# Gram products of the two heads side by side in the array's rows, and twelve slots for the experts' loaded tiles

## The chip, the core and the metric

The program runs on one core of a Trainium2 chip. The metric is the time of one execution on the device, in microseconds (us); lower is better. The core's engines run their own instruction streams and meet at semaphores: TensorE (PE, with the weight loads shown apart as PEld), VectorE (DVE), ScalarE (ACT), GpSimd (POOL), and SyncE (SP), which here issues nearly all loads. PE, DVE and ACT work out of two on-chip memories: SBUF, into which loads go, and PSUM, eight banks of 128 rows by 512 fp32 numbers, into which PE writes.

## The reference, cut to what matters

Two transformer blocks in fp32 run one behind the other on 256 tokens of width 1024. The change touches one stage in each. In the first block it is the mixture of experts, 4 groups of 8 experts, every expert with three matrices of 1024 x 256, 1024 x 256 and 256 x 1024:

```python
for g in range(N_GROUPS):
    hid = jax.nn.silu(jnp.einsum("bld,edf->blef", h, w_gate[g])) * jnp.einsum("bld,edf->blef", h, w_up[g])
    out = out + jnp.einsum("blef,ble,efd->bld", hid, comb[:, :, g], w_down[g])
```

`comb` is zero but for two experts of one group per token. In the second block it is the RWKV-7 mixer, a recurrence over tokens with 16 heads of 64. The kernel computes it in chunks of 128 tokens (two chunks, t = 0 and 1): products of decayed keys and queries within a chunk (the Gram products), the inverse of a triangular 128 x 128 matrix from them, and a 64 x 64 state per head that goes from the first chunk to the second.

## The kernel before

**Tiles of weights.** All large matrices are streamed through one ring in quarters of 128 x 1024 fp32 (512 KB). They are numbered through the program: `Q_MOE` = 84 is the first of the experts' 192, `Q_PLE` = 276 the first behind them. SP loads quarter n into a raw slot (`load`, L262). ACT writes its rounded high half to `whi` (`split_high`, L269), and DVE or POOL writes the rest to `wlo` (`split_low`, L275). `whi` and `wlo` have four slots. PE then does three products for one of fp32 (`times`, L282), at lines L284 to L286, and L1443 to L1445 for the experts' second matrix. Each product has 512 columns. The raw ring has four slots, and six during the experts (`MOE_RING`); the two more are carved from `proj`, whose end is free by then. `load` waits until the low half of the quarter that was in the slot is made: n - 6 for the experts, n - 4 elsewhere. So loads run six quarters, one expert, ahead of the splits. One semaphore per slot (`raw_full`) counts landed transfers; two transfers of 256 KB make one quarter of an expert.

**The experts.** The router's stage comes first (L1223 to L1376): norm, transposes, logits, a small product with `w_ple`, the choice of tokens. ACT issues seven loads for it after the last product of the first mixer (`router_loads`, L1210). `sp_experts` (L1190) issues the first four quarters, waits for the first quarter of the output product, and loops over the groups. For expert E, PE does gate and up of expert E+1 (four quarters), turns the hidden tile of E with two transposes (L1431), and then does down of E (two quarters). ACT copies the turned hidden tile (L1511) and does the silu (L1507); DVE splits all 192 quarters and multiplies. Once per group of 8 experts the tokens of the next group are gathered (L1387, `dve_gather`, L1409) and the group's result is scattered back (L1493, L1501).

**The heads.** `pe_heads`, `act_heads` and `dve_heads` (L2204, L2414, L2528) work on eight pairs of heads, the first by itself (`first`), six in a loop and the last by itself. A `step` (L2319) inverts for pair p in seven levels: `below` (L2254, masked by DVE at L2595) and `grow` (L2268 and L2272, copied by ACT at L2439 and L2440). Between the levels it does the tail of pair p-1 (`rest`, `solve`, `state`, `outputs`) and prepares pair p+1: `decays` (L2210), `turn_ar`, `turn_bk`, and behind `grow` of level 5 and `below` of level 6 the two calls of `grams` (L2238). The heads of a pair lie on rows 0 to 63 and 64 to 127 of `AR` and `BK`. A unit is one head and one chunk, numbered 2h + t, so the first call has both chunks of head 0 and the second those of head 1. Units alternate between banks 5 and 4, and each of the second call waits until DVE has masked the unit that was in its bank. DVE's `mask_grams` (L2573) does two units at L2576 and then two steps on both (L2585, L2588), the second of which the next pair's `below` of level 0 waits for. `decays` of the next pair waits for all four masks, since it writes bank 4. DVE's order is: mask level 5, centre pair p-1, mask units 0 and 1, mask level 6, mask units 2 and 3.

The pair's state is `SB`, 128 x 128 with a block for each head. In the second chunk `rest` and `outputs` multiply by it, 64 columns for each head at a time (L2284, L2312). For pair 0, `first` puts the two calls of `grams` behind the quarters 5 and 6 of the projection of the convolution (`Q_CONV`). The last loads ahead of the heads are three rows at L1802, which DVE waits for ahead of step 0 (`rows_loaded`).

## Time and profile before

| | us |
|---|---|
| three timed runs, median | 1567.47 (1564.97 to 1572.5) |
| the profiled execution | 1559.74 |
| its span, from the first to the last instruction | 1557.9 |
| PE busy | 1395.5 |
| DVE busy | 867.3 |
| ACT busy | 723.3 |
| POOL busy | 609.6 |
| experts' stage (about 394 to 735 us) | 341 |
| head pairs in the pattern (about 1064 to 1251 us) | 187 |

The profile takes one execution. A line of a timeline gives start, length, engine, line of the kernel, operation, what is written and read, and how many instructions of a kind follow one another (x8); in brackets stands how long the engine had been idle and whose end released it. Matmuls are pipelined: the recorded length of one reaches over the start of the next, so a time per product is read from starts. An fp32 product that isn't split is recorded as two passes; 64x256 is 64 rows of the array and 256 columns. The granted clock of TensorE is given as a share of 2.4 GHz; its two levels are 1.0 and 0.5.

### The profile page before, as it was taken

How to read it: one execution, taken by the hardware profiler on the slowest of the kernel's cores; microseconds unless marked ns; L12 is line 12 of the kernel's file. 1: busy time of each engine (PE TensorE's matmuls, PEld its weight loads, DVE VectorE, ACT ScalarE, POOL GpSimd, SP SyncE). 2: the span in 40 equal slices, each digit the busy share in tenths (PEclk: the TensorE clock that was granted, in tenths of full speed). 3: DMA queues.
4: the chain of work that ended last, by engine and by line, in shares of the span. 5: the costliest groups of instructions: out<-in, count | busy, mean ns of one | idle time of the engine just before them, and what ended most of it. 6: DMA issues, size and time to landing. Idle time of an engine off the chain costs nothing. (4 is left out here: it accounts for less than half of the span.)

```text
span 1557.9 us, 20851 instructions
## 1 busy us (share of the span) xinstructions
PE 1395.5 (90%) x6912; PEld 1138.3 (73%) x6912; DVE 867.3 (56%) x1436; ACT 723.3 (46%) x1209; POOL 609.6 (39%) x324
## 2 busy tenths in 40 slices
PE   5989987798899999997599999669999998799996
PEld 4877876676776767775477777558999986678885
DVE  2383353436688878885413999965666655211112
ACT  4455465434576767575543235352323323444442
POOL 5857658240000000001666566522000005578784
PEclk9999997699899999997899998979999998999998
DMA  6646533044597989985465365411000005355562
GB/s 206 182 119 183 148 120 107 0 135 160 182 344 274 341 289 328 314 295 171 121 199 156 108 199 160 143 54 55 2 0 0 0 1 176 108 162 177 173 188 81
DMA packets 127254, 239.92 MB, mean 154 GB/s; under 512 B 16296, under 2 KB 32346, under 8 KB 127056
## 3 DMA queue, kind: packets, MB, share of 16 engines
q1 hardware_dynamic: 116384, 227.12, 45.6%
q10 hardware_dynamic: 10801, 11.89, 2.7%
q8 instruction: 41, 0.67, 0.2%
q14 instruction: 28, 0.23, 0.1%
HBM read 234.79 MB, written 1.05 MB: 151 GB/s over the span
## 5 line engine op out<-in xcount | busy, mean ns | idle before, releaser
L278 POOL TENSOR_TENSOR wlo<-raw,whi 128x1024 fp32r<-128x1024 f32 (+1 forms) x232 | 567.0, 2464 | 711.6 <-ACT whi L273 711.1
L273 ACT ACTIVATE whi<-raw 128x1024 fp32r<-128x1024 f32 (+1 forms) x364 | 375.1, 1053 | 287.8 <-PE bank L286 218.6
L284 PE MATMUL bank<-whi,t0h 128*128 128x512 f32 (+1 forms) x1072 | 440.6, 411 | 23.0 <-DVE wlo L278 7.4
L285 PE MATMUL bank<-wlo,t0h 128*128 128x512 f32 (+1 forms) x1072 | 427.9, 399 | 0.0
L286 PE MATMUL bank<-whi,t0l 128*128 128x512 f32 (+1 forms) x1072 | 427.2, 398 | 0.0
L284 PEld LDWEIGHTS bank<-whi,t0h 128*128 128x128 f32 x1072 | 206.1, 192 | 83.7 <-issue 22.8
L286 PEld LDWEIGHTS bank<-whi,t0l 128*128 128x128 f32 x1072 | 205.6, 192 | 48.5
L285 PEld LDWEIGHTS bank<-wlo,t0h 128*128 128x128 f32 x1072 | 205.7, 192 | 44.6 <-issue 1.8
L278 DVE TENSOR_TENSOR wlo<-raw,whi 128x1024 fp32r<-128x1024 f32 x132 | 156.8, 1221 | 23.7 <-ACT whi L273 22.6
L356 PE MATMUL bank<-const,work 128*128 128x128 f32 x128 | 27.3, 402 | 66.4 <-DVE work L444 55.2
L2036 DVE SCALAR_TENSOR_TENSOR bank<-work,proj,bank 128x256 f32<-128x256 f32 x203 | 84.8, 483 | 1.9
L2513 POOL TENSOR_TENSOR proj<-proj,small x8 | 5.1, 637 | 205.0 <-PE bank L2314 205.0
L2595 DVE TENSOR_TENSOR work<-bank,const 128x256 f32<-128x256 f32 x112 | 46.7, 423 | 63.9 <-PE bank L2254 61.6
L278 DVE TENSOR_TENSOR wlo<-proj,whi 128x1024 fp32r<-128x1024 f32 x64 | 75.5, 1217 | 0.8 <-ACT whi L273 0.7
L273 ACT ACTIVATE whi<-proj 128x1024 fp32r<-128x1024 f32 x64 | 67.5, 1056 | 17.3 <-DMA proj<-in_w_exp_up 10.3
L356 PEld LDWEIGHTS bank<-const,work 128*128 128x128 f32 x128 | 24.4, 215 | 69.6 <-DVE work L444 41.0
L2885 DVE TENSOR_TENSOR t1l<-bank,t1h 128x512 fp32r<-128x512 f32 x16 | 10.3, 686 | 112.3 <-ACT t1h L2842 112.3
L2439 ACT COPY work<-bank 128x128 f32<-128x128 f32 x80 | 21.4, 267 | 83.4 <-PE bank L2272 83.4
L2272 PE MATMUL bank<-work 128*128 128x64 f32 x384 | 57.6, 276 | 0.7 <-DVE work L2595 0.7
L1443 PE MATMUL bank<-whi,t1h 128*128 128x512 f32 x128 | 54.3, 425 | 2.8 <-DVE wlo L278 2.8
L2254 PE MATMUL bank<-work 128*128 128x128 f32 x384 | 55.6, 287 | 0.1
L2770 PE MATMUL bank<-whi,t1h 128*128 128x512 f32 x128 | 51.4, 401 | 2.1 <-DVE t1l L2885 2.1
(411 smaller groups left out, 2002.7 us busy)
## 6 DMA issues: line engine op xcount, KB each, us to landing
raw<-in_w_ff SPq DMA_DIRECT2D x64, 512.0 KB, 3.6
raw<-in_w_exp_down SPq DMA_DIRECT2D x124, 256.0 KB, 4.5
raw<-in_w_in SPq DMA_DIRECT2D x60, 496.0 KB, 3.7
raw<-in_w_in SPq DMA_DIRECT2D x56, 512.0 KB, 3.6
raw<-in_w_exp_gate SPq DMA_DIRECT2D x66, 256.0 KB, 4.9
raw<-in_w_exp_up SPq DMA_DIRECT2D x66, 256.0 KB, 5.7
proj<-in_w_exp_gate SPq DMA_DIRECT2D x62, 256.0 KB, 4.4
proj<-in_w_exp_up SPq DMA_DIRECT2D x62, 256.0 KB, 5.4
```

What stands on the lines that cost most here:

```text
L273: nc.scalar.activation(whi[:, s, 0:width], raw_of(n)[:, 0:width], ACT.Copy).then_inc(hi_ready, 1)
L278: ins = (nc.vector if split_by_vector(n) else nc.gpsimd).tensor_tensor(wlo[:, s, 0:width], raw_of(n)[:, 0:width], whi[:, s, 0:width].bitca ...
L284: nc.tensor.matmul(dst, hi, wh, start=first, stop=False)
L285: nc.tensor.matmul(dst, hi, wl, start=False, stop=False)
L286: return nc.tensor.matmul(dst, lo, wh, start=False, stop=last)
L356: tr = nc.tensor.transpose(bank[4 + b][:, at:at + P], self.src[:, t, (2 * b + kk) * P:(2 * b + kk + 1) * P], ident)
L1443: nc.tensor.matmul(bank[4 + h][:, :], hh, whi[:, s, f], start=first, stop=False, skip_group_check=True)
L2036: ins = nc.vector.scalar_tensor_tensor(out=cvT[:, c, :] if w == W2 - 1 else partial(c), in0=uT[:, c, w:w + SEQ], scalar=tap, in1=partial(c ...
L2254: mm = nc.tensor.matmul(bank[g][:, v * P:(v + 1) * P], gram[b][:, u, 0:P], ident if lev == 0 else Xm[:, u, :], start=True, stop=True)
L2272: mm = nc.tensor.matmul(bank[2 + g][:, P + v * 64:P + (v + 1) * 64], Ym[:, u, :], odd[:, u], start=True, stop=True)
L2595: nc.vector.tensor_tensor((Xm if lev == 0 else Ym)[:, 2 * g:2 * g + 2, :], bank[g][:, 0:2 * P].rearrange("p (u s) -> p u s", u=2), con(f"l ...
L2770: nc.tensor.matmul(o, t1h[:, c, r], whi[:, s, f], start=False, stop=False, skip_group_check=True)
```

## The change

Two things are changed.

*Slots.* `MOE_RING` becomes 12. The six more slots are carved from `work` (columns 4864 to 11007). A new constant `PROJ_RING` = 6 keeps the old number where it meant which quarters DVE splits. Slots 6 to 11 have no semaphore of their own: `raw_event` gives them one that another stage has finished with, and the count that it has then. `load` and `split_high` go through it. The loads of the first group are written out, eight blocks, instead of six of them in a loop.

*Heads.* A unit is now 2t + h, so a call of `grams` has both heads of one chunk. Within a call the products go head 0, head 1, head 0, head 1; head 0 writes bank 5 and head 1 bank 4. The second call waits once, for both masks of the first. In `rest` and `outputs` the two products with `SB` for the second chunk are one of 128 columns, issued ahead of the heads' own.

```diff
--- before.py
+++ after.py
@@ -27,7 +27,8 @@
 TW = 512
 QF = 2 * TW
 RING = 4
-MOE_RING = 6
+MOE_RING = 12
+PROJ_RING = 6
 
 
 C_Z, C_XBC, C_DT, C_Q, C_K, C_V, C_GS, C_GA = 0, 1024, 2304, 2320, 3344, 4368, 5392, 6416
@@ -151,7 +152,7 @@
 
 def split_by_vector(n):
 
-    return Q_MOE - 2 <= n < Q_PLE or (Q_MOE - MOE_RING <= n < Q_MOE and n % 2 == 1)
+    return Q_MOE - 2 <= n < Q_PLE or (Q_MOE - PROJ_RING <= n < Q_MOE and n % 2 == 1)
 
 
 def slot(n):
@@ -173,7 +174,7 @@
 
     if not per:
         return counts[n]
-    span = JOB if per < JOB and JOB % per == 0 and n + JOB < Q_PLE and n >= Q_MOE - MOE_RING else per
+    span = JOB if per < JOB and JOB % per == 0 and n + JOB < Q_PLE and n >= Q_MOE - PROJ_RING else per
     return counts[n] + (counts[n + span] - counts[n]) * per // span * i
 
 
@@ -232,7 +233,7 @@
             return v.rearrange(f"p ({' '.join(names)}) -> p {' '.join(names)}", **dict(zip(names, shape)))
 
 
-        raw_full = [sem(f"raw_full{s}") for s in range(MOE_RING)]
+        raw_full = [sem(f"raw_full{s}") for s in range(PROJ_RING)]
         hi_ready = sem("hi_ready")
         lo_by_pool = sem("lo_by_pool")
         lo_by_dve = sem("lo_by_dve")
@@ -245,12 +246,23 @@
 
 
 
-        more_raw = proj[:, :, :].rearrange("p t n -> p (t n)")[:, 12232:12232 + (MOE_RING - RING) * QF]
+        more_raw = proj[:, :, :].rearrange("p t n -> p (t n)")[:, 12232:12232 + (PROJ_RING - RING) * QF]
+        work_raw = work[:, 4864:4864 + (MOE_RING - PROJ_RING) * QF]
 
         def raw_of(n):
 
             s = slot(n)
+            if s >= PROJ_RING:
+                return work_raw[:, (s - PROJ_RING) * QF:(s - PROJ_RING + 1) * QF]
             return raw[:, s, :] if s < RING else more_raw[:, (s - RING) * QF:(s - RING + 1) * QF]
+
+        def raw_event(n):
+
+            s = slot(n)
+            if s < PROJ_RING:
+                return raw_full[s], 0
+            return ((x_loaded, 16), (consts_loaded, 32), (vec_loaded, N_VEC), (sin_done, 2), (cb_done, 1),
+                    (x_split, 2 * NT))[s - PROJ_RING]
 
         def wait_low(eng, n, i=0, per=0):
 
@@ -264,11 +276,12 @@
             if before >= 0:
                 wait_low(sp, before, i, per)
             for dst, src in pairs:
-                sp.dma_start(dst, src).then_inc(raw_full[slot(n)], 16)
+                sp.dma_start(dst, src).then_inc(raw_event(n)[0], 16)
 
         def split_high(act, n, i=0, per=0, width=QF):
             s = n % RING
-            act.wait_ge(raw_full[slot(n)], at_turn(RAW_DONE, n, i, per))
+            full, loaded = raw_event(n)
+            act.wait_ge(full, at_turn(RAW_DONE, n, i, per) + loaded)
             wait_from(act, quarter_done, n - RING + 1 + per * i)
             nc.scalar.activation(whi[:, s, 0:width], raw_of(n)[:, 0:width], ACT.Copy).then_inc(hi_ready, 1)
 
@@ -1201,10 +1214,11 @@
             sp.wait_ge(quarter_done, Q_OUT + 1)
             for J in range(NG):
                 n = first_of(J)
-                with sp.Fori(0, 3) as i:
-                    for b in range(2):
-                        block(EG * J + 2 * i + b, n + 6 * b, i, U)
-                for e in (6, 7):
+                if J:
+                    with sp.Fori(0, 3) as i:
+                        for b in range(2):
+                            block(EG * J + 2 * i + b, n + 6 * b, i, U)
+                for e in (6, 7) if J else range(EG):
                     block(EG * J + e, n + 6 * e)
 
         def router_loads(act):
@@ -2186,7 +2200,7 @@
         head_var, head_root = sem("head_var"), sem("head_root")
 
         def unit(h, t):
-            return 2 * h + t
+            return 2 * t + h
 
         def halves(v, lev):
 
@@ -2228,16 +2242,17 @@
             def grams(p, c, units):
 
                 pe.wait_ge(*ft_copied.at(2 * p + 2))
-                for u in units:
-                    h, t = u // 2, u % 2
-                    if u >= 2:
-                        pe.wait_ge(*gram_masked.at(4 * p + u - 1))
-                    r = slice(64 * h, 64 * h + 64)
-                    ar = AR[c][r, t].rearrange("p a s -> p (a s)")
-                    for j in range(2):
-                        mm = nc.tensor.matmul(bank[5 - u % 2][:, 256 * j:256 * j + 256], BK[r, j, t, :], ar,
+                t = units[0] // 2
+                if t:
+                    pe.wait_ge(*gram_masked.at(4 * p + 2))
+                for j in range(2):
+                    for h in range(2):
+                        r = slice(64 * h, 64 * h + 64)
+                        ar = AR[c][r, t].rearrange("p a s -> p (a s)")
+                        mm = nc.tensor.matmul(bank[5 - h][:, 256 * j:256 * j + 256], BK[r, j, t, :], ar,
                                               start=True, stop=True)
-                    mm.then_inc(gram_done.sem, 1)
+                        if j:
+                            mm.then_inc(gram_done.sem, 1)
 
 
             def below(p, b, lev):
@@ -2278,12 +2293,11 @@
 
                 if t:
                     pe.wait_ge(s_ready, p + 1)
+                    nc.tensor.matmul(bank[6][:, 0:P], AR[c][:, 1, 0, :], SB, start=True, stop=False)
                 for h in range(2):
                     f = slice(h * DH, (h + 1) * DH)
-                    if t:
-                        nc.tensor.matmul(bank[6][:, f], AR[c][:, 1, 0, :], SB[:, f], start=True, stop=False)
                     mm = nc.tensor.matmul(bank[6][:, f], gram[c][:, unit(h, t), 256:384],
-                                          rkv[:, t, ds(2 * D + P * p + DH * h, DH)], start=t == 0, stop=True)
+                                          rkv[:, t, ds(2 * D + P * p + DH * h, DH)], start=t == 0, stop=t == 0 or h == 1)
                 mm.then_inc(w_made.sem, 1)
 
             def solve(p, c, t):
@@ -2308,11 +2322,11 @@
                         pe.wait_ge(*pair_done.at(p))
                 f = slice(h * DH, (h + 1) * DH)
                 oh = bank[7][:, t * P + h * DH:t * P + (h + 1) * DH]
-                if t:
-                    nc.tensor.matmul(oh, AR[c][:, 1, 1, :], SB[:, f], start=True, stop=False)
+                if t and h == 0:
+                    nc.tensor.matmul(bank[7][:, P:2 * P], AR[c][:, 1, 1, :], SB, start=True, stop=False)
                 nc.tensor.matmul(oh, gram[c][:, unit(h, t), 128:256], Uo[:, t, f], start=t == 0, stop=False)
                 mm = nc.tensor.matmul(oh, gram[c][:, unit(h, t), 384:512],
-                                      rkv[:, t, ds(2 * D + P * p + DH * h, DH)], start=False, stop=True)
+                                      rkv[:, t, ds(2 * D + P * p + DH * h, DH)], start=False, stop=t == 0 or h == 1)
                 if t == 1 and h == 1:
                     mm.then_inc(o_made.sem, 1)
 
```

## Rows read from the trace of the kernel before

**Rows 1.** Page: busy time of each engine over the span
```profile
PE 1395.5 (90%) x6912; PEld 1138.3 (73%) x6912; DVE 867.3 (56%) x1436; ACT 723.3 (46%) x1209; POOL 609.6 (39%) x324
```
**Rows 2.** Busy time by stretch: length, engines, PEclk, DMA share, GB/s
```profile
247.00:311.00 64.00, 48.41 (x250) 41.28 (x249) 27.49 (x85) 28.71 (x95) 32.39 (x73) 0.65 0.06 18
394.00:735.00 341.00, 317.33 (x1345) 241.53 (x1346) 270.24 (x290) 220.40 (x265) 4.99 (x2) 0.97 0.85 290
1064.00:1251.00 187.00, 185.57 (x1473) 174.40 (x1474) 117.20 (x283) 55.90 (x215) 10.40 (x13) 1.00 0.01 3
```
**Rows 3.** Instructions grouped, experts' stage: busy us, mean ns | idle before
```profile
L284 PE MATMUL bank<-whi,t0h 128*128 128x512 f32 x256 | 108.4, 423 | 9.6 <-DVE wlo L278 7.4 <-DVE t0l L1409 2.1
```
**Rows 4.** Timeline of PE in the experts' stage, three of its idle places
```profile
404.25 0.47 PE L284 MATMUL bank<-whi,t0h 128*128 128x512 f32 x1 [2.21 <-DVE wlo L278]
...
450.80 0.50 PE L284 MATMUL bank<-whi,t0h 128*128 128x512 f32 x1 [0.83 <-DVE wlo L278]
...
473.00 0.47 PE L284 MATMUL bank<-whi,t0h 128*128 128x512 f32 x1 [0.76 <-DVE wlo L278]
```
**Rows 5.** Timeline of ACT in the experts' stage
```profile
435.49 0.38 ACT L1511 ACTIVATE t1h<-bank 128x256 fp32r<-128x256 f32 x1 [1.24 <-PE bank L1431]
...
444.26 0.38 ACT L1511 ACTIVATE t1h<-bank 128x256 fp32r<-128x256 f32 x1 [0.48 <-PE bank L1431]
...
447.65 1.06 ACT L273 ACTIVATE whi<-proj 128x1024 fp32r<-128x1024 f32 x1 [0.95 <-DMA proj<-in_w_exp_up]
```
**Rows 6.** Busy time by stretch, columns as in rows 2: experts without a stall
```profile
415.00:445.00 30.00, 30.00 (x133) 23.58 (x132) 26.28 (x28) 21.92 (x27) 0.00 (x0) 1.00 0.98 340
```
**Rows 7.** Timeline of SP and PE around the router
```profile
354.52 1.08 SPq L267 DMA_DIRECT2D proj<-in_w_exp_gate  x1
...
374.31 0.66 PE L1273 MATMUL bank<-const,proj 128*128 128x128 f32 x4
```
**Rows 8.** Timeline of PE, end of a step and start of the next
```profile
1163.60 1.99 PE L2238 MATMUL bank<-work 64*128 64x256 f32 x8
1165.52 1.16 PE L2254 MATMUL bank<-work 128*128 128x128 f32 x8
1166.60 1.99 PE L2238 MATMUL bank<-work 64*128 64x256 f32 x8
1168.53 1.10 PE L2272 MATMUL bank<-work 128*128 128x64 f32 x8
1169.47 0.61 PE L2285 MATMUL bank<-proj,work 128*128 x4
1169.91 0.66 PE L2210 MATMUL bank<-proj,const 128*128 x4
```
**Rows 9.** Timeline of PE: products of two heads' halves in the attention
```profile
262.47 0.60 PE L1075 MATMUL bank<-work 64*128 64x256 f32 x4
262.90 0.49 PE L1074 MATMUL bank<-work 64*128 64x128 f32 x4
```
**Rows 10.** Timeline of DVE in the step of rows 8
```profile
1164.76 0.69 DVE L2576 TENSOR_TENSOR work<-bank,const 128x512 f32<-128x512 f32 x1 [0.66 <-PE bank L2238]
1165.62 0.69 DVE L2576 TENSOR_TENSOR work<-bank,const 128x512 f32<-128x512 f32 x1 [0.17 <-PE bank L2238]
...
1167.15 0.75 DVE L2595 TENSOR_TENSOR work<-bank,const 128x256 f32<-128x256 f32 x2
...
1169.82 0.42 DVE L2588 TENSOR_TENSOR work<-work,const 128x256 f32<-128x256 f32 x1
```
**Rows 11.** Timeline ahead of step 0, and the landing times of L1802's loads
```profile
1062.41 0.33 SPq L1802 DMA_DIRECT2D raw<-in_ln_x_b  x1
...
1063.70 1.28 DVE L2683 TENSOR_TENSOR proj<-proj,bank 128x512 f32<-128x512 f32 x2 [0.58 <-PE bank L286]
...
1065.04 0.71 PE L2210 MATMUL bank<-proj,const 128*128 128x128 f32 x4 [1.38 <-DVE proj L2683]
...
DMA to landing us min/median/max: 3.4/3.5/3.7
```

## The prediction

> **What bounds the kernel now.** I read the page first [rows 1]: over the span TensorE (PE) is busy nine tenths of the time, VectorE (DVE) and ScalarE (ACT) about half, so the question for each part of the change is whether PE waits there. The profiled execution took 1559.74 us: a span of 1557.9 and 1.8 outside it. The median of the three timed runs is 1567.47, 7.7 above it. The sum below is made in the profile's own time and then moved by that 7.7.
>
> The busy time by stage comes next [rows 2]. The change touches two stages. In the experts' 341 us DVE has 270 us of work and ACT 220, and PE is idle for 24. In the seven steps over head pairs from 1064 to 1251 us PE is busy 185.6 of 187 us, while DVE has 117 and ACT 56: PE is the bound, with hardly a gap. Here the DMA engines are unused.
>
> For the experts I then read the idle time ahead of their first product [rows 3] and its largest gaps on the timeline [rows 4]. An expert without a stall takes 8.77 us, from one copy of the turned hidden tile to the next [rows 5]. Its loads are six tiles of 524,288 bytes, 3.15 MB, so PE's pace asks for 359 GB/s. Where the DMA engines are busy 0.98 of the time they give 340 [rows 6], which is 9.25 us per expert. Six slots are one expert ahead, so this shortage of 0.48 us per expert soon reaches ACT, which at 447.65 had waited 0.95 us for a tile [rows 5]. Most such waits stop at ACT, since four split tiles stand between it and PE. Over the whole stage DMA isn't the limit: 192 tiles are 100.7 MB, 296 us at 340 GB/s, below 341.
>
> **Part A, twelve slots.** *What can go.* PE's waits for a low half at L284 sum to 7.4 us [rows 3], in ten places. One, 2.21 us at 404 us, is the first expert's [rows 4]: ACT there does the silu in program order ahead of the next splits, and no load is missing. Three of 0.76 (the one at 473.00 is shown) follow a gather, when DVE has its 1.22 us low half of the gathered rows to make. The remaining six add up to 7.4 - 2.21 - 2.28 = 2.9 us; the first, 0.83 at 450.80 [rows 4], comes right after ACT's wait of 0.95 for DMA [rows 5]. A matmul is recorded about 0.4 us long [rows 3], but 36 of them and two transposes fit in 8.77, about 0.23 each, so each gap hides some 0.17 us more of lost issue: 2.9 + 6 x 0.17 = 3.9 us. PE's wait near the stage's end, at L1443, is the last expert's chain from transpose to copy to split, and stays.
>
> *Does the supply suffice?* Now twelve tiles are ahead at the start. Each unstalled expert eats 0.31 tiles more than DMA brings (0.16 MB), 2.5 in a group of eight. But 32 experts at 8.77 are 281 of the 341 us: in the other 15 us of each group (gather, scatter, start) DMA brings more than it lacks. Six more tiles cover a group. I take the whole 3.9 us.
>
> The Trainium skill ("DMA: Bandwidth & Descriptors", Specifications) puts the limit of HBM per core at about 358 GB/s. By that figure a load would keep PE's pace almost exactly and a deeper ring would be needed little; the measured 340 decides here. The sum of part A would be the same 3.9 us at most.
>
> *What it adds.* The ring's first wait is now for a tile twelve back, so SP issues Q_MOE+4 to +11 in one go from 354.5 us, where it issued two and then stood until the first split of the router's end. Six tiles (3.1 MB) then share the rings with the seven loads that ACT issues from 349.8 on, 1.9 MB in all. Even if all six went ahead of them (5 MB, 14.7 us at 340 GB/s from about 357) they would be there by 372, and PE first needs them at 374.31 [rows 7]. Zero, and up to 2 us if SP's issue is slower. The loads go to `work` above the router's scratch. The eight blocks of the first group are written out instead of looped: 0 on SP, which is idle there. Waits on another semaphore cost the same. DVE and ACT behind SP wait for nothing new. Ends: a gain of 0 if the DMA engines stay the bound, 6.7 if the three waits after gathers go too (3 x 0.93). I take -3.9.
>
> **Part B1, Gram products.** Per pair there are two calls of `grams`, each four products that the profile shows as eight passes of 64x256. A call starts at 1163.60 and the next work at 1165.52: 1.92 us [rows 8]. All eight lie in one half of the array's rows. What two halves do together the attention shows, where the products of two heads lie in different halves: four passes of 256 columns start at 262.47 and the next ones at 262.90, 0.43 us or 0.108 each [rows 9]. So the two heads' passes run side by side, and four pairs of passes replace eight: 4 x 0.216 = 0.86 us less per call, 1.06 left, 1.73 per pair. That is what PE's own time loses. It is not what the pair loses, because the masks on DVE don't get shorter:
>
> 1. Today DVE masks the first unit at 1164.76 and the second at 1165.62, when each is done [rows 10]. With the halves side by side both are done when the first is today. The masks run behind one another: 1164.76, then 0.61 later (0.69 less the 0.08 by which DVE's instructions overlap, as in the two L2595 in 0.75 us), to 1166.06.
> 2. PE comes to the second call at 1166.60 - 0.86 = 1165.74. Its wait is now for both masks: 1166.06 + 0.06 (PE starts at 1065.04, 0.06 after DVE's two at 1063.70 end [rows 11]) = 1166.12. Wait 0.38.
> 3. After it, grow of level 6 would start at 1167.18. It needs the level-6 mask, which DVE does after L2585 and L2588, 0.25 us earlier than today's 1167.15: ended at 1167.31. Start 1167.37, wait 0.19, against 1168.53 today [rows 8]: 1.16 earlier.
> 4. The decays of the next pair (1169.91 today [rows 8]) need all four masks. DVE reaches the third at 1167.56 and ends the fourth at 1168.86; PE would be there at 1168.75 and starts at 1168.92. Wait 0.17, 0.99 earlier than today.
> 5. below of level 0 follows half a us later, 1169.42, and its second half at 1169.87 needs the last L2588 (1169.82 to 1170.24 today [rows 10]), which then ends at 1169.78. Just in time.
>
> So 0.73 of 1.73 come back as waits: 1.0 per pair, and seven such pairs (1 to 7, prepared in steps 0 to 6): -7.0. Behind the waiting PE instruction only the same pair's work is queued; who waits for it is DVE, which has its own queue to run. After step 5 DVE idles until PE's next product, so nothing is carried over.
>
> Pair 0 is prepared between quarters of the convolution's projection. There PE is the bound (POOL made the next quarters' low halves while earlier ones ran) and both masks are done before the second call, so 1.73 come off until L2683 at 1063.70. But DVE's first mask of step 0 also waits for the last of three rows: issued at 1062.41, landed up to 3.7 us later, 1066.1 [rows 11], hardly before that mask. Its issue hangs on a split that hangs on the quarter behind the first call alone, so it moves by 0.86. Gain 0.9.
>
> The Trainium skill ("TensorEngine Tiling (Array Packing)", PSUM Bottleneck) says that tiling speeds up TensorE but not the evacuation of PSUM, which may become the bottleneck. Steps 1 to 5 are that rule at this place; without it the sum would be 13.8 instead of 7.9.
>
> **Part B2, merged products with SB.** In `rest` and `outputs` of t=1 two products of 64 columns become one of 128. Four passes of 64 columns take 0.44 us, from 1169.47 to 1169.91, and eight of 128 take 1.08 with a change from and to 64 rows around them [rows 8], so 0.11 a pass for either width. Four passes fewer are 0.45 us per pair, on a PE without gaps there, and the copies that the next `below` needs end earlier than that. Seven pairs 3.15; in the last one DVE's scaling of the heads is the bound: 0.1. -3.2. Bounds 1.8 and 3.6.
>
> **The sum.** 3.9 + 7.0 + 0.9 + 3.2 = 15.0 us. Profiled: 1559.74 - 15.0 = 1544.7. Against the median: 1552.5.
>
> **Rivals.** *The masks are hidden* (DVE's chain shorter than I made it, or the clock gives something back): 13.8 + 3.6 + 3.9 to 6.6 = 21 to 24 us, 1546.2 to 1543.5. For: DVE has 10 us idle per pair. Against: the three waits follow one another in DVE's order. 0.15.
> *Loads stay the bound or the heads' waits are longer.* Part A gives 0 (0.98 busy at 340 GB/s [rows 6] speaks for it), 1556.4; or a pair gives 0.5, if DVE's chain is half a us longer than in steps 1 to 5: 1556.0; both, 1559.9. 0.22.
> *The halves don't run side by side* for these products. Then only B2 and A are left, 7.1 us, 1560.4, since the second call would find its masks done at 1166.5. Against: the attention shows the overlap on the same shape. 0.08. With A at 0 as well: 1564.3, 0.02.
> *The clock.* The head pairs run at a granted 1.00, that is 2.4 GHz [rows 2]. In the attention, where PE is busy 48 of 64 us, it is 0.65: seven tenths of the time at 1.2 GHz [rows 2]. If the new gaps let the clock fall, each us at the lower level costs half a us: 30 us of the 180 eat the whole gain, beyond 46 it is slower by over 0.5%, and a mean like the attention's makes 277 of the 180, 1650. The point from which it decides is PE's busy share; I leave it at 97% (0.73 of 25.5 us), and the experts with 93% were granted 0.97 [rows 2], so 0.03.
>
> **How the numbers follow.** Forecast 0.50 at 1552.5 (1549 to 1556), the rest as above. About 0.5%, 7.8 us, is what a measurement of this kernel can tell from no change; that is 1559.6. Faster by more: 0.50 + 0.15 + 0.19 = 0.84. Within: 0.12. Slower: 0.04. The range reaches over hidden masks, 1544, to products that don't overlap, 1561.
>
> **What would show it.** L2238: eight passes in about 1.06 us instead of 1.92. PE waits for L2576 ahead of the second call (about 0.4) and for L2595 (0.2), and one for L2576 ahead of L2210; none there shows the first rival. A pair in 25.5 instead of 27.0 us. In the experts, ACT's waits for DMA near zero and the stage about 337 us; the three waits of 0.76 and the 2.21 remain. The forecast is wrong if L2238 takes 1.9 us, if the granted clock in the pairs is below 1.00, or if ACT still waits for tiles.

## The result, and the profile after

The changed kernel takes 1544.24 us (median of 4 runs, 1541.33 to 1549.11), the kernel before 1566.5 in the same comparison (1564.97 to 1572.5): ratio 0.985, 95% interval 0.982 to 0.989. That is 23 us, between 17 and 29. A second comparison on another occasion (below) gave 0.9885, 0.985 to 0.992, or 18 us. The forecast was 15.

The profiled execution took 1549.11 us, a span of 1547.3 and 1.8 outside it, so only 10.6 less than the profiled one of before. I first look for those 10.6 us, stage by stage. Three rows of each kernel carry it: the transposes of the experts' hidden tiles (they start in the first expert and end in the last) and the Gram products and the products of `below`, which begin and end the work on head pairs. Columns: count, duration ns min/median/max, first and last start us, shapes. The kernel before:

```profile
L1431 PE MATMUL bank<-const,proj x64: 271/277/421, 408.2 to 714.2; 128*128 128x128 f32 x64
L2238 PE MATMUL bank<-work x128: 376/376/481, 1053.8 to 1249.2; 64*128 64x256 f32 x128
L2254 PE MATMUL bank<-work x384: 274/275/377, 1066.8 to 1273.6; 128*128 128x128 f32 x192
```

The changed kernel, where these lines are L1445, L2252 and L2269:

```profile
L1445 PE MATMUL bank<-const,proj x64: 271/276/284, 413.0 to 711.0; 128*128 128x128 f32 x64
L2252 PE MATMUL bank<-work x128: 375/376/481, 1053.4 to 1238.2; 64*128 64x256 f32 x128
L2269 PE MATMUL bank<-work x384: 274/275/378, 1065.1 to 1262.4; 128*128 128x128 f32 x192
```

The experts take 711.0 - 413.0 = 298.0 us where they took 306.0: 8.0 less. From the first Gram product to the last product of `below` it is 1262.4 - 1053.4 = 209.0 where it was 219.8: 10.8 less. Together 18.8. The rest of the program, which the change doesn't touch but for the loads ahead of the experts, gave 8.2 of it back in this pair of profiles: the start of the program to the first transposes 4.8 longer, from the last transposes to the first Gram product 2.8 (342.4 for 339.6), the end 0.6. Over the fourteen profiles of this study the rest of the program takes 832.1 to 844.2 us with the six slots of before and 835.3 to 843.9 with twelve, and the profile of before is the one with 832.1. So the 8.2 lie within what the rest varies by. I read the effect of the change from the two stages, and its total from the timed runs.

Against the forecast of 15.0, the head pairs came out about as summed (10.8 for 11.1; 9.6 to 10.8 in all the profiles with this edit), and the experts gave twice their term (8.0 for 3.9). The busy time by stretch, with the columns of [rows 2], for the head pairs and for the stretch of [rows 6]:

```profile
1064.00:1251.00 187.00, 182.51 (x1531) 171.04 (x1530) 118.28 (x290) 58.80 (x226) 9.73 (x13) 1.00 0.00 1
415.00:445.00 30.00, 29.91 (x130) 23.35 (x129) 26.72 (x28) 23.11 (x29) 0.00 (x0) 1.00 1.00 348
```

In the pairs PE now has gaps, 4.5 us in 187 instead of 1.4, and the granted clock stayed at 1.00, the 2.4 GHz level. The rival that feared for it is out; how many gaps it would take to lower the clock, no run here shows.

The end of one pair and the start of the next, PE's timeline (start, duration; in brackets idle time and what ended it). It answers to [rows 8]:

```profile
1137.66 0.37 PE L2224 MATMUL bank<-proj,const 128*128 x1
...
1157.92 1.14 PE L2252 MATMUL bank<-work 64*128 64x256 f32 x8
1158.99 1.16 PE L2269 MATMUL bank<-work 128*128 128x128 f32 x8
1160.43 1.13 PE L2252 MATMUL bank<-work 64*128 64x256 f32 x8 [0.29 <-DVE work L2590]
1161.76 1.10 PE L2287 MATMUL bank<-work 128*128 128x64 f32 x8 [0.19 <-DVE work L2609]
...
1163.31 0.71 PE L2224 MATMUL bank<-proj,const 128*128 x4
```

A call takes 1158.99 - 1157.92 = 1.07 us instead of 1.92. The products of `below` (L2269) take 1.08 before the second call, as L2254 did, so PE was there at 1160.07 and started at 1160.43: a wait of 0.36. The call done at 1161.50, growing of level 6 starts at 1161.76: 0.26. From there to the decays it is 1.55 us where it was 1.38 [rows 8]: 0.17. The pair takes 1163.31 - 1137.66 = 25.65 us; before, the decays at 1142.93 and 1169.91 were 26.98 apart.

DVE in the same stretch answers to [rows 10]. Both masks of a call now run behind one another (x2), as in the steps of the prediction:

```profile
1159.09 1.29 DVE L2590 TENSOR_TENSOR work<-bank,const 128x512 f32<-128x512 f32 x2 [0.66 <-PE bank L2252]
```

Now the experts, where the forecast was off. Groups of PE's instructions and of ACT's splits in the stage (busy us, mean ns | idle before and what ended it), the kernel before, beside [rows 3]:

```profile
L1493 PE MATMUL bank<-proj 128*128 128x512 f32 x32 | 15.3, 605 | 6.3 <-DVE xres L1501 4.9 <-DVE proj L1564 1.4
L273 ACT ACTIVATE whi<-raw 128x1024 fp32r<-128x1024 f32 x126 | 129.9, 1056 | 19.6 <-DMA raw<-in_w_exp_up 16.2 <-PE bank L1445 2.4 <-PE bank L286 0.9
L273 ACT ACTIVATE whi<-proj 128x1024 fp32r<-128x1024 f32 x64 | 67.5, 1056 | 17.3 <-DMA proj<-in_w_exp_up 10.3 <-PE bank L286 6.5
```

The changed kernel:

```profile
L297 PE MATMUL bank<-whi,t0h 128*128 128x512 f32 x256 | 106.8, 417 | 6.7 <-DVE wlo L291 4.5 <-DVE t0l L1423 2.1
L1507 PE MATMUL bank<-proj 128*128 128x512 f32 x32 | 15.3, 605 | 4.3 <-DVE xres L1515 2.9 <-DVE proj L1578 1.4
L286 ACT ACTIVATE whi<-work 128x1024 fp32r<-128x1024 f32 x96 | 97.9, 1054 | 5.1 <-PE bank L1459 5.1
L286 ACT ACTIVATE whi<-raw 128x1024 fp32r<-128x1024 f32 x64 | 65.8, 1056 | 5.2 <-PE bank L1459 5.1
L286 ACT ACTIVATE whi<-proj 128x1024 fp32r<-128x1024 f32 x32 | 33.7, 1053 | 6.6 <-PE bank L299 6.6
```

ACT waited 26.5 us for DMA and now not at all. PE's wait for low halves at L284 fell from 7.4 to 4.5, the 2.9 of the forecast: the places of 2.21 and three times 0.76 are left. Two things are here that the sum did not have. One is the scatter: PE's products at L1493 waited 4.9 us for DVE's additions, now 2.9.

The other is delay without an idle place. The busy time by stretch, cut at the first and the last transposes, columns as in [rows 2]; the kernel before, a second profile of it (`before_again`, below) and the changed kernel:

```profile
408.20:714.30 306.10, 295.88 (x1289) 227.03 (x1287) 255.44 (x271) 206.80 (x247) 0.00 (x0) 1.00 0.91 312
410.40:716.50 306.10, 296.07 (x1289) 226.22 (x1287) 256.48 (x272) 206.59 (x247) 0.00 (x0) 1.00 0.92 313
413.00:711.10 298.10, 292.85 (x1289) 227.43 (x1287) 253.22 (x272) 201.49 (x247) 0.00 (x0) 1.00 0.90 311
```

PE has the same 1289 instructions, but its idle time falls by 5.0 us (from 10.22 to 5.25) and its recorded busy time by 3.0. A product is recorded longer than the 0.23 us after which the next can start, so a product that comes up to some 0.17 us late only overlaps the one ahead of it less, and the record shows PE busy. In the same stretches the first product of a tile, L284, shows a part of it:

```profile
L284 PE MATMUL bank<-whi,t0h 128*128 128x512 f32 x244 | 102.1, 418 | 5.2 <-DVE wlo L278 5.2
L297 PE MATMUL bank<-whi,t0h 128*128 128x512 f32 x244 | 100.8, 413 | 2.3 <-DVE wlo L291 2.3
```

Its sum falls by 1.3, and that of the other groups of products changes by 0.3 at most. Of the 8.0 us, 2.9 are waits for low halves, 2.0 the scatter's, and 3.0 were hidden. The clock isn't behind it: the granted clock of the three stretches is 1.00. The first has 1.0 us at 1.2 GHz at its start, the second and the third none, and the second needs the same 306.0 us from transposes to transposes as the first.

### The profile page after: what moved, and what is told of

Same layout as the page of the kernel before. It is cut to its first block, busy times and chain, and to the rows that moved or that the text cites. A ratio compares the mean times of both kernels' runs of the same rounds, so it can differ in the third digit from the quotient of the medians.

```text
span 1547.3 us, 20663 instructions
## 1 busy us (share of the span) xinstructions
PE 1386.0 (90%) x6880; PEld 1130.7 (73%) x6880; DVE 861.6 (56%) x1436; ACT 718.1 (46%) x1209; POOL 608.3 (39%) x324
## 4 chain that ended last, share of the span: by engine, by line
PE 42%; issue 39%; POOL 9%; DVE 7%; ACT 2%; DMA 1%; POOLq 0%; DVEq 0%; ACTq 0%
POOL wlo L291 9%; PE bank L297 7%; PE bank L298 6%; PE bank L299 6%; PE bank L2269 3%; PE bank L2287 3%; PE bank L2283 2%; PE bank L2784 2%; PE bank L2786 2%; PE bank L2785 2%; DVE work L764 2%; PE bank L369 1%; PE bank L2252 1%; DVE work L457 1%; DVE work L998 1%
## 5 line engine op out<-in xcount | busy, mean ns | idle before, releaser
L286 ACT ACTIVATE whi<-raw 128x1024 fp32r<-128x1024 f32 (+1 forms) x300 | 309.3, 1053 | 280.8 <-PE bank L299 237.7
L291 DVE TENSOR_TENSOR wlo<-work,whi 128x1024 fp32r<-128x1024 f32 x96 | 113.0, 1218 | 7.5 <-ACT whi L286 7.4
L286 ACT ACTIVATE whi<-work 128x1024 fp32r<-128x1024 f32 x96 | 97.9, 1054 | 5.1 <-PE bank L1459 5.1
L291 DVE TENSOR_TENSOR wlo<-raw,whi 128x1024 fp32r<-128x1024 f32 x68 | 80.2, 1219 | 14.1 <-ACT whi L286 14.1
L1457 PE MATMUL bank<-whi,t1h 128*128 128x512 f32 x128 | 53.5, 418 | 2.9 <-DVE wlo L291 2.8
L2269 PE MATMUL bank<-work 128*128 128x128 f32 x384 | 55.6, 287 | 0.4 <-DVE work L2609 0.4
L2287 PEld LDWEIGHTS bank<-work 128*128 128x128 f32 x384 | 49.9, 192 | 4.8 <-issue 3.5
```

The source lines that it names most:

```text
L286: nc.scalar.activation(whi[:, s, 0:width], raw_of(n)[:, 0:width], ACT.Copy).then_inc(hi_ready, 1)
L291: ins = (nc.vector if split_by_vector(n) else nc.gpsimd).tensor_tensor(wlo[:, s, 0:width], raw_of(n)[:, 0:width], whi[:, s, 0:width].bitca ...
L1457: nc.tensor.matmul(bank[4 + h][:, :], hh, whi[:, s, f], start=first, stop=False, skip_group_check=True)
L2269: mm = nc.tensor.matmul(bank[g][:, v * P:(v + 1) * P], gram[b][:, u, 0:P], ident if lev == 0 else Xm[:, u, :], start=True, stop=True)
L2287: mm = nc.tensor.matmul(bank[2 + g][:, P + v * 64:P + (v + 1) * 64], Ym[:, u, :], odd[:, u], start=True, stop=True)
```

## The experiments

In each: the edit, what was expected (on record before the run), what was measured. "Experts" is the time from the first to the last start of the transposes, "pairs" from the first Gram product to the last product of `below`, both as above. The expectations of the `ahead` and `scatter` runs count the experts' time on a measure that is 6.1 to 6.2 us shorter (299.8 for 306.0, 292.0 for 298.1). Each ratio is against runs of the kernel before on the same chip. Each kernel has one profile, and "experts" varies between kernels with the same ring: 303.8 to 307.1 in the six with tiles six ahead and the scatter of before (grams_blocked 303.8, grams_only 307.1), 298.0 to 298.1 in the five with eight or twelve ahead.

**Both parts apart, and both kernels again.** `slots_only` has the ring of twelve and the heads of before, `heads_only` the other way round. The edits are the two halves of the diff shown above.

> The kernel before, unchanged, for a second profile. The profiles of before and after differ by 10.6 us, the timed medians by 22. If the difference is chance of the granted clock in stages that the change leaves alone, this profile's stages outside the experts and the heads will differ from the first profile's by several us (the first one's span was 1557.9), and its time will lie near 1566. In the experts' stage both theories (depth of the ring; clock) can be told apart here: if the half clock at the start (products 0.43 us apart at 405 to 409 us) and at the last expert (717 to 722) comes from chance, it will be absent or elsewhere; if it belongs to the kernel before, it will be there again.

> Only the twelve slots; the heads as before. My prediction had -3.9 us. Theory depth: the whole stage loses what late tiles cost, also in steps too small to be listed as idle and in the scatters that wait for a DVE that is behind: -8 to -9 us. Theory clock: beside that another 3.4 us came off in the profile because the clock was at 2.4 GHz in the first and last expert; if that belongs to the change it is -11 to -12 us. Rival that the heads gave more than the profile shows: -4 us here.

> Only the heads' part; six slots as before. From the steps of the prediction -11.1 us. If the time that the sum lacked is in the heads' part: -18 us. A pair takes 25.65 us instead of 26.99, and the experts' stage is that of the kernel before.

> Both parts, for a second profile and a narrower interval. If the parts are independent, the gains of slots_only and heads_only add up to this one, -20 to -23 us; if one hides the other, it is less than their sum.

| kernel | ratio (95%) | experts | pairs |
|---|---|---|---|
| before | | 306.0 | 219.8 |
| before_again | 1.000 (0.997 to 1.003) | 306.0 | 219.8 |
| slots_only | 0.9955 (0.9932 to 0.9978) | 298.1 | 219.9 |
| heads_only | 0.9952 (0.9926 to 0.9977) | 306.7 | 210.2 |
| after | 0.985 (0.982 to 0.989) | 298.0 | 209.0 |
| after_again | 0.9885 (0.985 to 0.992) | 298.1 | 209.8 |

Each part shortens its own stage and leaves the other's within its spread, and the stages add up. In the timed runs each part alone is worth 7 us (3 to 12 by the intervals), the two together 18, less than the 20 to 23 expected. The stages say 8 and 10. That the missing time was in the heads' part (18 us for it alone) is out. The other expectation that is answered here is the clock's: PE is at 1.2 GHz from 405.8 to 409.2 and from 716.4 to 723.2 in the first profile of before, and in before_again up to 402.4 and from 719.8. So where it falls is chance, it lies almost wholly outside the stretch of the transposes, and slots_only has its 8 us without it.

**Depth, or the place of the slots.** Twelve slots also bring new memory for six tiles, other semaphores, and a first group written out on SP. Two kernels keep all this and take back only the distance between a load and the low half that it waits for:

```diff
-            before = n - (MOE_RING if Q_MOE + RING <= n < Q_PLE else RING)
+            before = n - (6 if Q_MOE + RING <= n < Q_PLE else RING)
```

`ahead8` has an 8 there. This holds at the start of the stage too, so the remark in the first expectation, that the twelve tiles at the start remain, isn't so: SP stands behind the sixth tile in `ahead6` (the next load starts at 377.93 us) and behind the eighth in `ahead8` (380.08), where the changed kernel has issued twelve by 372.

> Heads as before; the experts' stage has its twelve slots, their memory and the written-out first group, but the load of tile n waits for the low half of tile n-6 again, so no more than six tiles are ahead (at the start of the stage still the twelve). Theory 'depth': what twelve slots bring is distance between load and use, so this kernel falls back to the kernel before: from the first expert to the last 299 to 301 us (before 299.8, slots_only 292.0), the scatter experts 14 to 15 us instead of 13.5, ACT waiting some 25 us for DMA in the stage, whole time within 0.3% of before. Rival 'place': the other memory, the other semaphores or the loop written out on SP bring the gain: 292 us and -0.45%. In between (295 to 298) if the twelve tiles at the start alone bring a part.

> As ahead6, but the load waits for the low half of tile n-8. Theory: the DMA engines fall short by 0.31 tiles per expert, so two tiles more cover some six experts of a group of eight, and the first experts behind gather and scatter are served anyway: most of the gain, from the first expert to the last 293 to 296 us; ACT's waits for DMA some 3 to 10 us. If depth doesn't matter but only the start or the memory does, the same value as ahead6.

The transposes of `ahead6`:

```profile
L1445 PE MATMUL bank<-const,proj x64: 270/276/284, 412.3 to 719.0; 128*128 128x128 f32 x64
```

and of `ahead8`:

```profile
L1445 PE MATMUL bank<-const,proj x64: 271/276/284, 414.6 to 712.7; 128*128 128x128 f32 x64
```

Experts 306.7 and 298.1 us; ratios 0.9993 (0.996 to 1.0025) and 0.993 (0.990 to 0.996). Six ahead is the kernel before, in time and in ACT's waits for DMA (25.5 us), whatever the memory, the semaphores and the written-out group. Eight ahead, with eight at the start, is all of the gain, so neither the last four slots nor the twelve tiles at the start bring anything that can be seen here. Theory "depth" holds, and its dose was over-estimated: expected were 293 to 296 us on that measure, which are 299 to 302 on this one, and 3 to 10 us of ACT's waits. ACT's waits for DMA in `ahead8`, all that is left of them:

```profile
L286 ACT ACTIVATE whi<-work 128x1024 fp32r<-128x1024 f32 x96 | 97.9, 1054 | 5.1 <-PE bank L1459 4.7 <-DMA work<-in_w_exp_up 0.3
```

The prediction put the shortage at 0.31 tiles per expert, from 340 GB/s at a DMA share of 0.98 [rows 6]. The same stretch in the changed kernel shows 348 GB/s at 1.00 (above), and in before_again:

```profile
415.00:445.00 30.00, 29.55 (x127) 22.73 (x126) 25.98 (x28) 21.76 (x27) 0.00 (x0) 1.00 1.00 349
```

At 349 the 3.15 MB of an expert take 9.0 us instead of 9.25, and the shortage against 8.77 is 0.16 tiles, 1.3 in a group of eight, by this estimate. Two more slots cover that. Over the fourteen profiles the stretch shows 340 to 357 GB/s, and the 340 of the prediction is the lowest.

**The scatter.** The 2.0 us at L1493 were a term that the sum had left out. In the six kernels named above this wait is 4.0 to 5.5 us, and 2.9 in the five. In program order DVE adds the scattered products behind the four low halves of the next expert's tiles; PE's fourth product reuses the bank of the first, and so waits for the first addition. The expert with the second group's scatter in before_again, first a split of ACT, then DVE, then PE on the timeline:

```profile
491.01 1.06 ACT L273 ACTIVATE whi<-proj 128x1024 fp32r<-128x1024 f32 x1 [1.14 <-DMA proj<-in_w_exp_up]
...
492.77 2.36 DVE L278 TENSOR_TENSOR wlo<-proj,whi 128x1024 fp32r<-128x1024 f32 x2
495.24 2.51 DVE L278 TENSOR_TENSOR wlo<-raw,whi 128x1024 fp32r<-128x1024 f32 x2
497.66 2.58 DVE L1501 TENSOR_TENSOR xres<-xres,bank 128x512 f32<-128x512 f32 x4
...
498.39 1.12 PE L1493 MATMUL bank<-proj 128*128 128x512 f32 x2 [2.29 <-DVE xres L1501]
```

and PE there in the changed kernel:

```profile
497.85 1.12 PE L1507 MATMUL bank<-proj 128*128 128x512 f32 x2 [0.97 <-DVE xres L1515]
```

A tile that came 1.14 us late made 2.29 of PE's wait where 0.97 are the order's own. To see how much of part A went this way, the fourth product gets a bank of its own, with six slots and with twelve; the wait is then at the next transposes, which use bank 2:

```diff
-                if z == 3:
-                    pe.wait_ge(x_added, 4 * J - 3)
-                nc.tensor.matmul(bank[(3, 6, 7, 3)[z]][:, :], ...
+                nc.tensor.matmul(bank[(2, 3, 6, 7)[z]][:, :], ...
...
-                o, o, bank[(3, 6, 7, 3)[z]][:, :]
+                o, o, bank[(2, 3, 6, 7)[z]][:, :]
...
             def turn_hidden(E, e_par, added=0):
                 pe.wait_ge(hid_ready, E + 3)
+                if added:
+                    pe.wait_ge(x_added, added)
```

> The same edit in the kernel before, with six slots. Theory: late tiles push DVE's four low halves together, the addition behind them comes late, and PE's fourth product pays 4 to 5 us in three scatters that twelve slots make 2.9 and no late tiles; without that wait the three experts with a scatter take 12.5 to 13.3 us instead of 14.0 to 15.7, from the first expert to the last 295.5 to 297.5 instead of 299.8. Rival: the late tiles themselves are the delay, and the wait only moves to the next low half: 14 us and more, 299 to 300.

> The changed kernel, with the four products that scatter a group's result in four different banks (2, 3, 6, 7 instead of 3, 6, 7, 3), so that the fourth doesn't wait for DVE's first addition; the next transposes into bank 2 wait for it instead. Theory: with twelve slots each of the three scatters inside the stage still holds PE 0.97 us at this wait, because the addition stands behind four low halves in DVE's order; the expert with a scatter falls from 13.50 to 12.5 us, the stage by 3 us. Rival: PE only comes earlier to DVE's next late output (hidden layer or its low half): 13.3 to 13.5 us.

The transposes and the scatter's products, with six slots:

```profile
L1433 PE MATMUL bank<-const,proj x64: 270/276/284, 412.4 to 711.9; 128*128 128x128 f32 x64
L1493 PE MATMUL bank<-proj 128*128 128x512 f32 x32 | 14.5, 595 | 1.4 <-DVE proj L1564 1.4
```

and with twelve:

```profile
L1447 PE MATMUL bank<-const,proj x64: 270/276/284, 411.5 to 705.9; 128*128 128x128 f32 x64
L1507 PE MATMUL bank<-proj 128*128 128x512 f32 x32 | 14.5, 595 | 1.4 <-DVE proj L1578 1.4
```

Experts 299.5 us with six slots (306.0 before) and 294.4 with twelve (298.0). The wait for the additions is gone in both and came back nowhere. The rival, that the late tiles are the delay and the wait only moves, is out. This edit alone, without a slot more, brings 6.5 us, more than expected (293.3 on that measure, for 295.5 to 297.5), where the slots bring 8.0; behind it the slots still bring 5.1. By these figures 2.9 us of the slots' 8.0 pass through this one wait. The 299.5 is a single profile and such kernels spread by 3.3 us, so I take 2.9 as an estimate, good to 1.5 or so; the fall of the wait itself, 2.0 us, agrees with it. In whole time `scatter_before` has a ratio of 0.994 (0.992 to 0.997). `scatter_after` has 0.9865 (0.983 to 0.990), which can't be told from the changed kernel's; its 3.6 us are shown by the stage alone.

**What the Gram products gained.** `grams_only` is `heads_only` without the merged products with SB. `grams_blocked` is `heads_only` with another order inside a call:

```diff
-                for j in range(2):
-                    for h in range(2):
-                        r = slice(64 * h, 64 * h + 64)
-                        ar = AR[c][r, t].rearrange("p a s -> p (a s)")
+                for h in range(2):
+                    r = slice(64 * h, 64 * h + 64)
+                    ar = AR[c][r, t].rearrange("p a s -> p (a s)")
+                    for j in range(2):
```

> Six slots, the Gram products on both halves of the rows, but the products with SB separate as in the kernel before. By the prediction's steps a pair takes 25.65 + 0.45 = 26.1 us (the changed kernel's 25.65, before 26.99), and the stretch from the first Gram product to the last product of the head pairs lengthens by 3 us against heads_only (210.2), to 213.2. Rival: the merging brings nothing, because DVE's waits behind it take it back: 25.7 and 210.5; or it brings more, as four passes fewer also spare waits: 26.4 and above.

> As heads_only (six slots, products with SB merged), but in each call the four passes of the lower half come first and then the four of the upper half, instead of taking turns. Theory 'two streams': the engine keeps order only within a half, so the order of issue matters little: call 1.07 to 1.2 us, pair 25.65 to 25.8. Rival 'turns': passes start in order of issue, so only neighbours of different halves overlap: four then four gives one overlap in the middle, call 1.7 to 1.9 us, second call later by 0.6 to 0.8, pair 26.4 to 27.0, some 5 to 9 us longer than heads_only.

In `grams_only` two decays in a row start at

```profile
1092.37 0.37 PE L2210 MATMUL bank<-proj,const 128*128 x1
...
1118.47 0.37 PE L2210 MATMUL bank<-proj,const 128*128 x1
```

A pair takes 26.10 us: the Gram products are worth 26.98 - 26.10 = 0.88, the merging 0.45. The pairs' stretch is 212.4 us, 2.2 above heads_only and 3.1 above grams_blocked, which have the same work. These two differ by 0.9, in the first step, at a wait of DVE for a load: 2.70 us in heads_only, 1.80 and 1.73 in the two others. The merging is worth 2.2 to 3.1 us in the stretch, for 3.2 forecast. Ratio 0.997 (0.994 to 0.9997).

`grams_blocked`, ratio 0.992 (0.990 to 0.995), pairs 209.3 us, a pair 25.65:

```profile
1136.87 1.14 PE L2238 MATMUL bank<-work 64*128 64x256 f32 x8
1137.94 1.16 PE L2255 MATMUL bank<-work 128*128 128x128 f32 x8
1139.38 1.14 PE L2238 MATMUL bank<-work 64*128 64x256 f32 x8 [0.28 <-DVE work L2576]
```

The call takes 1.07 us, as with alternating halves. The alternation named in the change does nothing of its own that can be seen here; both halves in one call is what counts.

**The chain of masks.** If the three waits of a pair are DVE's masks behind a second call that comes too early after the first, then the first call only has to come sooner. It is put between the two halves of growing of level 5, in the changed kernel:

```diff
-            def grow(p, b, lev):
+            def grow(p, b, lev, between=None):
...
+                    if g and between:
+                        between()
...
-                grow(p, b, 5)
-                if prep:
-                    grams(p + 1, c, (0, 1))
+                grow(p, b, 5, (lambda: grams(p + 1, c, (0, 1))) if prep else None)
```

> The changed kernel, with the first call of the Gram products put between the two halves of the growing of level 5, so that DVE gets the masks' input some 0.6 us of PE time earlier; no work is added or removed. Theory of the prediction's steps 1 to 4 (the three waits in the chain of masks are DVE's order behind an early second call): the waits of 0.28, 0.20 and 0.17 us vanish, a pair takes 25.0 instead of 25.65, seven pairs -4.5 us and the ratio to before some 0.003 below the changed kernel's. Rival: another DVE instruction (the level-6 mask or the copies behind level 5) then comes late, the same sum of waits stands at other lines, pair 25.6.

```profile
1101.23 1.13 PE L2252 MATMUL bank<-work 64*128 64x256 f32 x8
1102.29 0.66 PE L2285 MATMUL bank<-work 128*128 128x64 f32 x4
...
1104.39 1.13 PE L2252 MATMUL bank<-work 64*128 64x256 f32 x8
1105.46 1.10 PE L2289 MATMUL bank<-work 128*128 128x64 f32 x8
...
1107.00 0.71 PE L2224 MATMUL bank<-proj,const 128*128 x4
...
1132.14 0.37 PE L2224 MATMUL bank<-proj,const 128*128 x1
```

Two of the three waits are gone; from growing to the decays it is still 1.54 us, so the third, 0.16, stands. A pair takes 25.14 us (25.0 expected), the pairs' stretch 1254.9 - 1049.4 = 205.5, 3.5 less than the changed kernel's. Median 1540.1 us, ratio 0.983 (0.980 to 0.987), which can't be told from the changed kernel's; the gain is shown by the stage. The account of the waits holds for 0.51 of 0.79 us.

**Both edits on top of the change.**

> The changed kernel with both edits, earlier Gram products and scatter over four banks: pair 25.0 us, experts with a scatter 12.5; together 7 to 8 us less than the changed kernel, ratio to before about 0.981 to 0.984. If the pieces give nothing by their rivals, it is the changed kernel's 0.985 to 0.989.

Experts 294.4, pairs 205.5 us, median 1541.0, ratio 0.982 (0.979 to 0.985). It is the best ratio of the study, though in whole time it can't be told from `grams_earlier`; its stages are shorter than the changed kernel's by 3.6 and 3.5, together the 7 that was expected.

## Where the prediction held and where it failed

**The calls and the chain of masks (part B1) held.** 1.06 us per call was forecast and 1.07 measured; waits of 0.38, 0.19 and 0.17 against 0.36, 0.26 and 0.17; 1.0 us per pair against 0.88. Of 1.71 us taken from PE's products, 0.79 came back as waits. The trace agrees here with the rule of the Trainium skill ("TensorEngine Tiling (Array Packing)", PSUM Bottleneck) that tiling speeds up TensorE and not what empties PSUM. Pair 0: the load of the last row, whose landing was said to bound the gain, does. In the kernel before nothing waited for it, in the changed one DVE does and PE behind it:

```profile
1061.14 0.33 SPq L1816 DMA_DIRECT2D raw<-in_ln_x_b  x1
...
1064.65 0.76 DVE L2609 TENSOR_TENSOR work<-bank,const 128x256 f32<-128x256 f32 x2 [1.59 <-DMA raw<-in_ln_x_b]
```

From the first Gram product to the first product behind it (L2254's, L2269's group of 384) it is 13.0 us before, 11.7 in after, 12.5 in after_again, 12.9 in heads_only: a gain of 0.1 to 1.3, with the landing, for 0.9 forecast.

**The merging (B2) held**: 0.45 per pair.

**The failed step is part A's term, 3.9 us for 8.0**, in the sentence "The remaining six add up to ... 2.9", with 0.17 for each as all that a gap hides. The 2.9 were right. What was missing:
- The wait of the scatter's fourth product, 4.9 us at a line that I hadn't looked at, was taken as part of the work. 2.0 of it came from late tiles. The experiment with its own bank puts what passes there at 2.9, from single profiles.
- Delays that leave no idle place. 0.17 times six was 1.0, where PE's recorded busy time fell by 3.0 with the same instructions. Besides the six gaps there were, by this reading, delays too short to leave any gap; which products they held is not told apart.

So 8.0 is 2.9 + 2.0 + 3.0, where the sum had 2.9 + 1.0. Most of part A was in what the list of PE's idle time at one line doesn't hold. The bound above, 6.7, was built from the wrong piece: the three waits after gathers, which stayed, as the forecast said.

**The supply step** had the right direction and too large a shortage (0.31 tiles per expert for about 0.16), which changed nothing in the sum but hid that eight slots would do. The added loads at the start cost nothing that can be told from what that stretch varies by: the first transposes start at 408.2 to 414.3 us in the six kernels with six slots (before, before_again, heads_only, grams_only, grams_blocked, scatter_before), and at 411.5 to 414.6 in the eight with twelve (of which ahead6 and ahead8 load only six and eight tiles early).

**The total.** 15.0 forecast; 18.8 in the two stages; 23 (17 to 29) and 18 (12 to 24) in the two timed comparisons. The stages account for the second and lie inside the interval of the first. What the first shows beyond them, some 4 us, is not tied to any place in the program, and I leave it as the spread of the runs: the runs of the kernel before in the second comparison lie between 1554.8 and 1574.5. The measured median lies in the range of the first rival, hidden masks, but its mechanism isn't there: all three waits for masks stand in the rows. That its number fits is chance. The rival in which loads stay the bound is out too, since ACT no longer waits for them.

## What to carry to other kernels

When a late transfer is to be removed, don't sum the idle time at the line that reads the data: compare the length of the whole stage, and of each repetition, with the undisturbed one, and count every wait of the bottleneck engine whose releaser sits behind the late work in another engine's queue. A wait that a queue's order makes (a product that reuses a bank whose reader stands behind other work) passes on the delays ahead of it in that queue; a free bank can be worth nearly as much as a deeper ring. And before doubling a ring, work out the dose: here two slots more did what six did.

## What the runs showed of the hardware

**Order of products in the two halves of the rows.** In `grams_blocked` four passes of one half are issued and then four of the other, and all eight take 1.07 us; in one half alone, eight take 1.92 [rows 8]. PE's timeline, cut 0.18 us behind the start of a call, already has two passes in it:

```profile
1136.87 0.49 PE L2238 MATMUL bank<-work 64*128 64x256 f32 x2
```

In the kernel before, where all lie in one half, passes start 0.216 us apart or more. So the second of these is the first of the other half, which is issued fifth. If passes started in the order of issue, that couldn't be, and the second four would follow the start of the fourth, 3 x 0.216 = 0.65 us in, and end 0.86 later, at 1.5 (an estimate). So PE ran them as two streams. The Trainium skill ("TensorE: Matmul & The Clock Gate", The mechanism) says that matmuls start and end strictly in the order of the program, without reordering; for products in different halves these rows do not agree. Whoever lets one signal on the last product stand for all of them should keep that in mind.

**DVE and POOL stand in each other's way.** Far from the change, 24 operations of DVE on two inputs in SBUF, 128x256 each, take 0.47 us apiece, or 2.6 when one of POOL's low halves is running. In the profile of after, eight of them fell on one, in that of after_again four; first after, where POOL's second block of low halves came between them:

```profile
849.54 26.75 DVE L2033 SCALAR_TENSOR_TENSOR proj<-proj,mul 128x256 f32<-128x256 f32 x24
...
863.67 2.40 POOL L291 TENSOR_TENSOR wlo<-raw,whi 128x1024 fp32r<-128x1024 f32 x1 [2.53 <-ACT whi L286]
```

and after_again, where that block (four in 11.80 us) began when DVE was nearly done, and was itself held up:

```profile
850.32 18.20 DVE L2033 SCALAR_TENSOR_TENSOR proj<-proj,mul 128x256 f32<-128x256 f32 x24
...
865.99 11.80 POOL L291 TENSOR_TENSOR wlo<-raw,whi 128x1024 fp32r<-128x1024 f32 x4 [4.08 <-ACT whi L286]
```

The Trainium skill ("SBUF — State Buffer", Terms) calls it a port pair with an exclusive lock, held for the whole instruction, whose loser stands still; the two durations agree. Seven of the fourteen profiles have the long form (26.0 to 26.8 us for the 24), seven the short one (18.2), and the same kernel shows both. From the last transposes to the first Gram product the former take 342.3 us in the mean, the latter 338.8. This is 3.5 us of what differs between two profiles of one kernel. The long form is in one of six kernels with six slots and in six of eight with twelve; whether the ring shifts the odds, through the moment at which the stage begins, stays open.
